# Opening of a hybrid decoder trunk: the first scale and shift as columns, and x turned ahead of them

## Chip, cores and metric

The kernel runs on one core of a Trainium2 chip. The metric is the device time of one launch in microseconds; smaller is better.

## The reference, cut to what matters

A trunk of two layers, each of three sub-layers (a SwiGLU feed-forward, a hybrid mixer, a second feed-forward), on 256 tokens of 1024 features in float32. Every sub-layer starts with the same two steps. The change touches them for the first feed-forward only:

```python
mod = silu(c) @ w_ada[i] + b_ada[i]                       # c is one vector of 1024
sh1, sc1, g1, ... = split(mod, 9)
h = rms_norm(x, norm_pre[i, 0]) * (1 + sc1) + sh1         # by token: x / rms(x), by feature: the rest
y = swiglu_ffn(h, w_ffn_in[i, 0], w_ffn_out[i, 0])
```

## The kernel before, in words

**Products.** Every large product is made of three products of rounded float32 (fp32r): a weight chunk (128x1024 in RAW) is split by ScalarE into a high half (WH, line 1348) and by VectorE into the rest (WL, line 1697), and activations likewise into HH and HL; high by high, high by low and low by high are summed in PSUM. TensorE needs 12 products of 512 columns for a chunk.

**The opening.** The first feed-forward goes through its first 12 chunks in the order FIRST_ORDER (lines 76 and 77): for each quarter q of the 1024 input features, the chunks of units 0, 1 and 2. So chunks 3q, 3q+1 and 3q+2 need only quarter q of h. Quarter q of scale and shift needs 16 slabs of w_ada (8 blocks of 128 rows, for scale and for shift), which the SP queue loads in pieces (`first_slabs`, line 682) between the weight chunks: chunks 2q and 2q+1 go out beside the slabs of quarter q.

**Scale and shift as rows.** `first_rows_of` (line 999) multiplies two or four of the eight row blocks on TensorE with the activated c as a stationary operand broadcast over 128 columns, so that each partition of PSUM bank 7 holds the same 512 numbers (256 of shift, 256 of scale). The other blocks are accumulated by VectorE in `first_steps` (line 1716, operations at line 1729), and one product with ones (line 1008) adds their sum over partitions. The norm's gain is spread over partitions by four one-row products (line 1317) at the very start.

**h by token.** VectorE makes x times root times gain (`first_x_pre`, line 1735), then for each quarter (1 + scale) times that (line 1748, twice) plus shift (line 1753, twice). TensorE turns the result by four transposes (`first_turn`, line 1019), ScalarE copies it rounded into HH (line 1423), and VectorE subtracts HH from the turned block for HL (line 1761). The turns of quarters 1 to 3 stand ahead of the last products of chunks 2, 5 and 8.

**Order.** All of it is written out by hand: each engine has its own program and waits on semaphores. VectorE: roots, steps of quarter 0, h of quarter 0, then for each quarter w_lo to chunk 3q, HL, w_lo of chunk 3q+1, steps of the next quarter, w_lo of chunk 3q+2, h of the next quarter (lines 2261 to 2280). ScalarE: squares and roots of x, a table load, then w_hi to chunk 3q and HH for each quarter. TensorE fills its waits ahead of the first chunk with products of ones (`kept_busy`, line 1309: 8, 6 and 1 of them). ACC and PSLAB hold sums and slabs; X and Y hold x and h by token. Eight chunks can be in RAW; SP issues chunk g + 8 when chunk g was used.

Of the kernel before, what the change touches and what calls it, by code (L numbers as in the profile page):

```python
# [11 lines left out]
ALU = mybir.AluOpType  # L12
# [305 lines left out]
def build(nc, x_d, c_d, w_ada, b_ada, norm_pre, norm_post, w_ffn_in, w_ffn_out, w_in, pool_w, w_ret_out, w_pool_out,  # L318
          w_ssm_out, w_fox_out, w_out, vecs_d, consts_d, out_d):
    with ExitStack() as ctx:  # L320
# [47 lines left out]
        EPS = SMALL[:, 16:17]  # L368
        DUMMY = SMALL[:, 17:18]
        _, dg_off = sb("rows_area", [P, TT, P])  # L370
        ZF = at("dt_by_feature", [P, T], F32, dg_off)
# [86 lines left out]
        def scaled(b, n):  # L458

            return n if b == 0 else 2 + 5 * (b - 1) + n  # L460

# [19 lines left out]
        first_used = sem("ada_first_used")  # L481
        first_rows = sem("first_rows_in_psum")
        first_pre = sem("first_pre_row_landed")
        first_pre_ps = sem("first_pre_row_in_psum")
        late_h = sem("late_h_by_token")
        ada_used = Signal(sem("ada_used"), 24)
# [129 lines left out]
        def _(sp):  # L616
# [50 lines left out]
            def pre_row(t):  # L667
                if t == 1:
                    sp.wait_ge(late_h, 6)
                else:  # L670
                    sp.wait_ge(f_ok, scaled(t - 1, 5))
                sp.dma_start(AROW[:], norm_pre[t // 3, t % 3, :].partition_broadcast(P)).then_inc(pre_landed.sem, 16)
# [18 lines left out]
            sp.dma_start(CS[:], c_d.rearrange("a (k p) -> p (a k)", p=P)).then_inc(c_landed, 16)  # L691
            sp.dma_start(AROW[0:1, :], norm_pre[0, 0:1, :]).then_inc(first_pre, 16)
            for tt in range(TT):
# [5 lines left out]
            first_slabs(0, 2)  # L699
            sp.dma_start(KC[:, 0:P], consts_d[:, 0:P]).then_inc(ident_landed, 16)  # L700
            for q in range(4):
                if q:
                    first_slabs(q, 0)
                chunk(2 * q)
                if q:
                    first_slabs(q, 1)
                chunk(2 * q + 1)
# [33 lines left out]
        def _(pe):  # L741
# [9 lines left out]

            def token_chunk(g, j, banks, hi, lo, kn, tts, lo_ready=None, ahead_of_last=None):

# [24 lines left out]
                for kk, tt in parts:  # L778
                    k = 2 * j + kk
                    if ahead_of_last is not None and (kk, tt) == parts[-1]:  # L780
                        ahead_of_last()
                    out = PS[:, banks + tt, :]
                    cs = slice(kk * HALF, (kk + 1) * HALF)
                    mm(out, hi[:, k, tok(tt)], wh[:, cs], start=(k == 0), stop=False)  # L784
                    mm(out, hi[:, k, tok(tt)], wl[:, cs], start=False, stop=False)  # L785
                    if lo_ready is None:
                        ins = lo_product(kk, tt)
# [6 lines left out]
            def ffn_in(s, c):  # L794
# [44 lines left out]
                if s == 0 and u == 0:  # L839
                    pe.wait_ge(hh_ok, h_parts(0, q + 1))  # L840

                    def ready():
                        pe.wait_ge(hl_ok.sem, hl_ok.at(0, q + 1))
                ahead = None
                if s == 0 and c in (2, 5, 8):
                    def ahead():
                        first_turn(c // 3 + 1)
                token_chunk(g, q, unit_banks(s, u), HH, HL, KD, (0, 1), ready, ahead).then_inc(w_used, 1)

# [148 lines left out]

            def first_rows_of(q):

                out = PS[:, 7, :].rearrange("p (n c) -> p n c", n=2)
                slabs = PSLAB[:].rearrange("p (n k) c -> p n k c", n=2)
                for i, k in enumerate(on_pe(q)):
                    pe.wait_ge(ada_first[piece_of(q, k)], 32)
                    mm(out, CS[:, k:k + 1].to_broadcast([P, P]), slabs[:, :, k, q * QUARTER:(q + 1) * QUARTER], start=(i == 0),
                       stop=False)
                pe.wait_ge(first_used, first_steps_of(q)[1])
                mm(out, ones, ACC[:, 0:2 * D].rearrange("p (n c) -> p n c", n=2)[:, :, q * QUARTER:(q + 1) * QUARTER],
                   start=False, stop=True).then_inc(first_rows if q < 3 else a_ps.sem, 1)

            def first_turn(q):

                for tt in range(TT):
                    if q == 0:
                        pe.wait_ge(f_ok, scaled(0, tt + 1))
                    else:
                        pe.wait_ge(late_h, 2 * (q - 1) + tt + 1)
                    for k in range(2):
                        ins = pe.transpose(PS[:, 6, k * T + tt * P:k * T + (tt + 1) * P],
                                           Y[:, tt, (2 * q + k) * P:(2 * q + k + 1) * P], ident)  # L1020
# [11 lines left out]
            def ffn(s):  # L1032
# [3 lines left out]
                for c in range(4 if s else 0, N_IN):  # L1036
# [3 lines left out]
                    if s == 0 and c in (2, 5, 8):  # L1040
                        first_rows_of(c // 3 + 1)
                    if s == 0 and c == 27:
# [271 lines left out]

            pe.wait_ge(first_pre, 16)
            for half in range(2):
                ins = mm(PS[:, 2 + half, :], ONE[0:1, 0:1].to_broadcast([1, P]), AROW[0:1, half * HALF:(half + 1) * HALF],
                         start=True, stop=True)
            ins.then_inc(first_pre_ps, 1)
            kept_busy(8)  # L1320
            first_rows_of(0)
            pe.wait_ge(xsq_ok.sem, xsq_ok.at(0, 4))
            pe.wait_ge(ident_landed, 16)
            kept_busy(6)
            first_turn(0)
            kept_busy(1)
            for s in range(SUBS):
# [7 lines left out]
        def _(act):  # L1335
# [83 lines left out]

            def first_h_hi(q):  # L1420

                act.wait_ge(t_ps, h_parts(0, q + 1))
                fn(HH[:, 2 * q:2 * q + 2, :], PS[:, 6, :].rearrange("p (k t) -> p k t", k=2), ACT.Copy).then_inc(hh_ok, 1)

# [245 lines left out]
            x_square(0, 0)  # L1670
            x_square(0, 1)
            fn(DUMMY[:], one, ACT.Silu)
            for q in range(4):
                split_to(3 * q)
                first_h_hi(q)
            for s in range(SUBS):
# [7 lines left out]
        def _(dve):  # L1684
# [30 lines left out]

            def first_steps(q):

                cs = slice(q * QUARTER, (q + 1) * QUARTER)
                acc = ACC[:, 0:2 * D].rearrange("p (n c) -> p n c", n=2)[:, :, cs]
                slabs = PSLAB[:].rearrange("p (n k) c -> p n k c", n=2)  # L1720
                if q == 0:
                    for n in range(2):
                        dve.wait_ge(bias_landed[n].sem, bias_landed[n].at(0, 16))
                for m in range(*first_steps_of(q)):
                    k = FIRST_STEPS[m][1]
# [5 lines left out]

            def first_x_pre(tt):

                dve.wait_ge(first_pre_ps, 1)
                chain(dve.scalar_tensor_tensor(Y[:, tt, :].rearrange("p (b n) -> p b n", b=2),
                                               X[:, tt, :].rearrange("p (b n) -> p b n", b=2), RB[:, tt:tt + 1],
                                               PS[:, 2:4, :], ALU.mult, ALU.mult))

            def first_h_full(q):

                cs = slice(q * QUARTER, (q + 1) * QUARTER)
                if q < 3:
                    dve.wait_ge(first_rows, q + 1)
                else:
                    dve.wait_ge(a_ps.sem, a_ps.at(0, 1))
                scaled_at = []
                for tt in range(TT):
                    ins = dve.scalar_tensor_tensor(Y[:, tt, cs], PS[:, 7, QUARTER:2 * QUARTER], 1.0, Y[:, tt, cs], ALU.add,
                                                   ALU.mult)
                    scaled_at.append(chain.mark(ins))  # L1750
                for tt in range(TT):
                    chain.need(scaled_at[tt])
                    dve.tensor_tensor(Y[:, tt, cs], Y[:, tt, cs], PS[:, 7, 0:QUARTER], ALU.add)\
                        .then_inc(late_h if q else f_ok, 1)
                if q == 3:
                    dve.sem_inc(a_ok.sem, 1)

            def first_h_lo(q):

                dve.wait_ge(hh_ok, h_parts(0, q + 1))  # L1760
                dve.tensor_tensor(HL[:, 2 * q:2 * q + 2, :], PS[:, 6, :].rearrange("p (k t) -> p k t", k=2),
                                  HH[:, 2 * q:2 * q + 2, :], ALU.subtract).then_inc(hl_ok.sem, 1)
# [498 lines left out]
            for tt in range(TT):  # L2261
                x_part(0, tt)
                x_root(0, tt)
                if tt == 0:
                    first_x_pre(0)
            first_steps(0)
            first_x_pre(1)
            first_h_full(0)
            for q in range(4):
# [4 lines left out]
                split_to(3 * q + 1)  # L2274
                first_steps(q + 1)
                split_to(3 * q + 2)
                if q == 2:
                    dve.wait_ge(first_used, len(FIRST_STEPS))
                    dve.sem_inc(ada_used.sem, ADA_FIRST)
                first_h_full(q + 1)  # L2280
            for s in range(SUBS):
# [108 lines left out]
```

## Time and profile before

| what | value |
|---|---|
| median of 3 runs | 1488.42 us (1487.47 to 1488.42) |
| the profiled execution, its own time | 1487.86 us |
| its span, first to last instruction | 1485.8 us |
| TensorE, VectorE, ScalarE, GpSimd busy | 99%, 78%, 55%, 4% |
| DMA | 342.94 MB, mean 231 GB/s |
| first product of chunk 0 | 17.93 us after the span's start |
| first product of chunk 9 (the last quarter of h) | 53.63 us |

The profiled execution takes 2.06 us more than its span, and 0.56 us less than the median. PE is TensorE, PEld its weight loads, DVE VectorE, ACT ScalarE, POOL GpSimd, SP the DMA queue. A product of 512 columns shows 0.39 us long, since its pipeline is included; what counts is the spacing of starts.

### The profile page before, as it was taken

What the parts mean: (1) busy time and instruction counts of PE and PEld (TensorE: products, weight loads), DVE (VectorE), ACT (ScalarE), POOL (GpSimd) and SP (SyncE); (2) the same over time, 40 slices, a digit from 0 to 9 for tenths busy, and PEclk for the clock granted to TensorE, in tenths of its full rate; (3) what the DMA queues carried; (4) which work ended last, traced back from release to release, by engine and by line L of the source; (5) the groups of instructions that cost most, each with busy time, mean ns of one, the idle gap of its engine ahead of it and who ended that gap; (6) DMA issues with size and microseconds to landing.
All of it is one profiled execution on the core that took longest, in us unless ns stands there. A gap on an engine that the chain in (4) does not pass through costs nothing.

```text
span 1485.8 us, 20504 instructions
## 1 busy us (share of the span) xinstructions
PE 1473.5 (99%) x7991; PEld 1259.6 (85%) x7991; DVE 1161.1 (78%) x1414; ACT 816.5 (55%) x1016; POOL 56.8 (4%) x56
## 2 busy tenths in 40 slices
PE   8999999999999999999999999999999999999998
PEld 5788889997988878888888888899888888888886
DVE  6888777867799878889787897776879988775663
ACT  4545465566563456556465564654746545664553
POOL 0000003200000000000000000050000000000000
PEclk9999999999999999999999999999999999999999
DMA  9899966556777847888768887665667787566652
GB/s 349 292 323 303 336 221 206 167 164 186 226 250 245 284 156 241 259 277 286 241 227 263 272 280 250 192 184 158 183 192 244 244 263 234 179 187 186 195 187 99
DMA packets 203623, 342.94 MB, mean 231 GB/s; under 512 B 18547, under 2 KB 118131, under 8 KB 203526
## 3 DMA queue, kind: packets, MB, share of 16 engines
q1 hardware_dynamic: 185382, 275.56, 58.2%
q10 hardware_dynamic: 18144, 66.07, 13.4%
q8 instruction: 63, 1.03, 0.3%
q14 instruction: 34, 0.28, 0.1%
HBM read 340.53 MB, written 1.05 MB: 230 GB/s over the span
## 4 chain that ended last, share of the span: by engine, by line
PE 97%; DVE 2%; ACT 1%; issue 1%; DMA 0%; DVEq 0%; ACTq 0%
PE ps L819 12%; PE ps L784 11%; PE ps L775 11%; PE ps L785 11%; PE ps L933 6%; PE ps L935 6%; PE ps L934 6%; PE ps L824 6%; PE ps L1274 5%; PE ps L1275 5%; PE ps L1276 5%; PE ps L867 3%; PE ps L973 1%; PE ps L860 1%; PE ps L1146 1%
## 5 line engine op out<-in xcount | busy, mean ns | idle before, releaser
L1697 DVE TENSOR_TENSOR w_lo<-w_raw,w_hi 128x1024 fp32r<-128x1024 f32 x480 | 574.7, 1219 | 100.7 <-ACT w_hi L1348 100.2
L1348 ACT ACTIVATE w_hi<-w_raw 128x1024 fp32r<-128x1024 f32 x490 | 504.7, 1051 | 259.5 <-DMA w_raw<-in_w_ffn_out 70.5
L784 PE MATMUL ps<-w_hi,h_both 128*128 128x512 f32 x586 | 231.0, 394 | 0.0
L785 PE MATMUL ps<-w_lo,h_both 128*128 128x512 f32 x586 | 228.3, 390 | 0.0
L775 PE MATMUL ps<-w_hi,h_both 128*128 128x512 f32 x586 | 227.6, 390 | 0.0
L819 PE MATMUL ps<-h_both,w_hi 128*128 128x512 f32 x768 | 206.6, 394 | 0.0
L1274 PE MATMUL ps<-h_both,w_hi 128*128 128x256 f32 x640 | 182.6, 285 | 0.0
L1276 PE MATMUL ps<-h_both,w_lo 128*128 128x256 f32 x640 | 181.1, 283 | 0.0
L1275 PE MATMUL ps<-h_both,w_hi 128*128 128x256 f32 x640 | 181.1, 283 | 0.0
L1713 DVE SCALAR_TENSOR_TENSOR ada_acc<-ada_slab,c_silu,ada_acc 128x1024 f32<-128x1024 f32 x128 | 163.7, 1279 | 5.7 <-DMA ada_slab<-in_w_ada 5.7
L819 PEld LDWEIGHTS ps<-h_both,w_hi 128*128 128x128 f32 x768 | 132.9, 189 | 19.2
L933 PE MATMUL ps<-w_hi,act_hi 128*128 128x512 f32 x352 | 137.6, 391 | 0.0
L935 PE MATMUL ps<-w_hi,act_lo 128*128 128x512 f32 x352 | 137.0, 389 | 0.0
L934 PE MATMUL ps<-w_lo,act_hi 128*128 128x512 f32 x352 | 137.0, 389 | 0.0
L784 PEld LDWEIGHTS ps<-w_hi,h_both 128*128 128x128 f32 x586 | 110.1, 188 | 24.1 <-DVE w_lo L1697 2.4
L775 PEld LDWEIGHTS ps<-w_hi,h_both 128*128 128x128 f32 x586 | 110.0, 188 | 23.4
L785 PEld LDWEIGHTS ps<-w_lo,h_both 128*128 128x128 f32 x586 | 110.2, 188 | 21.8
L824 PEld LDWEIGHTS ps<-h_both,w_lo 128*128 128x128 f32 x768 | 114.5, 189 | 14.2
L1274 PEld LDWEIGHTS ps<-h_both,w_hi 128*128 128x128 f32 x640 | 122.7, 192 | 0.6 <-issue 0.3
L1275 PEld LDWEIGHTS ps<-h_both,w_hi 128*128 128x128 f32 x640 | 122.8, 192 | 0.2
L1276 PEld LDWEIGHTS ps<-h_both,w_lo 128*128 128x128 f32 x640 | 122.7, 192 | 0.0
L824 PE MATMUL ps<-h_both,w_lo 128*128 128x256 f32 x768 | 118.3, 281 | 0.0
(310 smaller groups left out, 1860.2 us busy)
## 6 DMA issues: line engine op xcount, KB each, us to landing
w_raw<-in_w_ffn_in SPq DMA_DIRECT2D x352, 256.0 KB, 3.8
w_raw<-in_w_in SPq DMA_DIRECT2D x168, 512.0 KB, 3.7
ada_slab<-in_w_ada ACTq DMA_DIRECT2D x126, 512.0 KB, 4.6
w_raw<-in_w_ffn_out SPq DMA_DIRECT2D x88, 512.0 KB, 4.2
w_raw<-in_w_ssm_out SPq DMA_DIRECT2D x16, 512.0 KB, 4.7
w_raw<-in_w_out SPq DMA_DIRECT2D x16, 512.0 KB, 3.4
ada_slab_first<-in_w_ada SPq DMA_DIRECT2D x14, 512.0 KB, 7.2
w_raw<-in_w_pool_out SPq DMA_DIRECT2D x8, 512.0 KB, 3.6
```

The lines of the kernel that those rows point to most:

```text
L775: return mm(PS[:, banks + tt, :], lo[:, k, tok(tt)], wh[:, kk * HALF:(kk + 1) * HALF], start=False, stop=(k == kn - 1))
L784: mm(out, hi[:, k, tok(tt)], wh[:, cs], start=(k == 0), stop=False)
L785: mm(out, hi[:, k, tok(tt)], wl[:, cs], start=False, stop=False)
L819: ins = mm(PS[:, bank, :], wh[:, cs], HB[:, k, :, :], start=(k == 0), stop=(k == KD - 1))
L824: ins = mm(PS[:, bank, 0:T], wl[:, cs], HH[:, k, :], start=False, stop=False)
L933: mm(out, hi[:, k, tok(tt)], wh[:, cs], start=first, stop=False)
L934: mm(out, hi[:, k, tok(tt)], wl[:, cs], start=False, stop=False)
L1274: mm(out, wh[:, cs], HH[:, k, :], start=(k == 0 and t % 2 == 0), stop=False)
L1275: mm(out, wh[:, cs], HL[:, k, :], start=False, stop=False)
L1276: ins = mm(out, wl[:, cs], HH[:, k, :], start=False, stop=(k == KD - 1 and t % 2 == 1))
L1348: fn(WH[:, n % N_HI, 0:width], RAW[:, n % N_RAW, 0:width], ACT.Copy).then_inc(w_hi, 1)
L1697: dve.tensor_tensor(WL[:, n % N_RAW, 0:width], RAW[:, n % N_RAW, 0:width], WH[:, n % N_HI, 0:width], ALU.subtract).then_inc(w_lo, 1)
```

## The change

Scale and shift become columns, one number for each partition (feature). TensorE takes the slab as the stationary operand and the activated c as one moving column: for each row block of a quarter four products, for shift and scale by two feature blocks of 128, into 16 columns of bank 7. x times root is made by ScalarE, turned by TensorE without waiting for scale and shift, and full h is made from the turned block with a scale and a bias for each partition: high half and full h by ScalarE (high half of quarter 0 by VectorE), into HH and into Y, which is free by then. The gain is loaded as 1024 single elements (NORMC) behind the identity, and the load of its row is dropped.

```diff
@@ -367,6 +367,9 @@
         DUMMY = SMALL[:, 17:18]
+        NORMC, _ = sb("first_norm_columns", [P, KD])
+        SCALEC, _ = sb("first_scale_columns", [P, KD])
+        SHIFTC, _ = sb("first_shift_columns", [P, KD])
         _, dg_off = sb("rows_area", [P, TT, P])
...
@@ -457,7 +460,7 @@
-            return n if b == 0 else 2 + 5 * (b - 1) + n
+            return 5 * (b - 1) + n
...
@@ -665,9 +670,7 @@
             def pre_row(t):
-                if t == 1:
-                    sp.wait_ge(late_h, 6)
-                else:
+                if t > 1:
                     sp.wait_ge(f_ok, scaled(t - 1, 5))
...
@@ -689,7 +692,6 @@
             sp.dma_start(CS[:], c_d.rearrange("a (k p) -> p (a k)", p=P)).then_inc(c_landed, 16)
-            sp.dma_start(AROW[0:1, :], norm_pre[0, 0:1, :]).then_inc(first_pre, 16)
             for tt in range(TT):
...
@@ -698,6 +700,7 @@
             sp.dma_start(KC[:, 0:P], consts_d[:, 0:P]).then_inc(ident_landed, 16)
+            sp.dma_start(NORMC[:], norm_pre[0, 0:1, :].rearrange("a (k p) -> p (a k)", p=P)).then_inc(first_pre, 16)
             for q in range(4):
...
@@ -841,11 +842,7 @@
                         pe.wait_ge(hl_ok.sem, hl_ok.at(0, q + 1))
-                ahead = None
-                if s == 0 and c in (2, 5, 8):
-                    def ahead():
-                        first_turn(c // 3 + 1)
-                token_chunk(g, q, unit_banks(s, u), HH, HL, KD, (0, 1), ready, ahead).then_inc(w_used, 1)
+                token_chunk(g, q, unit_banks(s, u), HH, HL, KD, (0, 1), ready).then_inc(w_used, 1)
...
@@ -996,25 +993,29 @@
-            def first_rows_of(q):
-
-                out = PS[:, 7, :].rearrange("p (n c) -> p n c", n=2)
-                slabs = PSLAB[:].rearrange("p (n k) c -> p n k c", n=2)
-                for i, k in enumerate(on_pe(q)):
+            def column_group(q):
+
+                return [(PS[:, 7, 4 * q + 2 * n + b:4 * q + 2 * n + b + 1], n, q * QUARTER + b * P) for n in range(2)
+                        for b in range(2)]
+
+            def first_products_of(q, ks):
+
+                for k in ks:
                     pe.wait_ge(ada_first[piece_of(q, k)], 32)
-                    mm(out, CS[:, k:k + 1].to_broadcast([P, P]), slabs[:, :, k, q * QUARTER:(q + 1) * QUARTER], start=(i == 0),
-                       stop=False)
+                    for i, (out, n, col) in enumerate(column_group(q)):
+                        mm(out, PSLAB[:, 8 * n + k, col:col + P], CS[:, k:k + 1], start=(k == 0 and i == 0), stop=False)
+
+            def first_sums_of(q):
+
                 pe.wait_ge(first_used, first_steps_of(q)[1])
-                mm(out, ones, ACC[:, 0:2 * D].rearrange("p (n c) -> p n c", n=2)[:, :, q * QUARTER:(q + 1) * QUARTER],
-                   start=False, stop=True).then_inc(first_rows if q < 3 else a_ps.sem, 1)
+                for i, (out, n, col) in enumerate(column_group(q)):
+                    ins = mm(out, ACC[:, n * D + col:n * D + col + P], one, start=False, stop=(i == 3))
+                ins.then_inc(first_sums if q < 3 else a_ps.sem, 1)
...
+                pe.wait_ge(x_rooted, 4 if q else 2)
                 for tt in range(TT):
-                    if q == 0:
-                        pe.wait_ge(f_ok, scaled(0, tt + 1))
-                    else:
-                        pe.wait_ge(late_h, 2 * (q - 1) + tt + 1)
                     for k in range(2):
...
@@ -1038,7 +1039,9 @@
                     if s == 0 and c in (2, 5, 8):
-                        first_rows_of(c // 3 + 1)
+                        first_turn(c // 3 + 1)
+                        first_products_of(c // 3 + 1, on_pe(c // 3 + 1))
+                        first_sums_of(c // 3 + 1)
                     if s == 0 and c == 27:
...
@@ -1312,18 +1315,15 @@
-            pe.wait_ge(first_pre, 16)
-            for half in range(2):
-                ins = mm(PS[:, 2 + half, :], ONE[0:1, 0:1].to_broadcast([1, P]), AROW[0:1, half * HALF:(half + 1) * HALF],
-                         start=True, stop=True)
-            ins.then_inc(first_pre_ps, 1)
-            kept_busy(8)
-            first_rows_of(0)
-            pe.wait_ge(xsq_ok.sem, xsq_ok.at(0, 4))
+            kept_busy(14)
+            first_products_of(0, (0, 1))
+            kept_busy(3)
+            first_products_of(0, (4,))
             pe.wait_ge(ident_landed, 16)
-            kept_busy(6)
             first_turn(0)
-            kept_busy(1)
+            first_products_of(0, (6,))
+            first_sums_of(0)
+            kept_busy(3)
             for s in range(SUBS):
...
@@ -1417,10 +1417,29 @@
-            def first_h_hi(q):
+            def first_by_root(tt, c0, c1):
+
+                act.wait_ge(first_roots, tt + 1)
+                fn(Y[:, tt, c0:c1], X[:, tt, c0:c1], ACT.Copy, scale=RB[:, tt:tt + 1]).then_inc(x_rooted, 1)
+
+            def first_h(q):
...
                 act.wait_ge(t_ps, h_parts(0, q + 1))
-                fn(HH[:, 2 * q:2 * q + 2, :], PS[:, 6, :].rearrange("p (k t) -> p k t", k=2), ACT.Copy).then_inc(hh_ok, 1)
+                act.wait_ge(first_columns, q + 1)
+                for b in range(2):
+                    k = 2 * q + b
+                    if q:
+                        ins = fn(HH[:, k, :], PS[:, 6, b * T:(b + 1) * T], ACT.Identity, scale=SCALEC[:, k:k + 1],
+                                 bias=SHIFTC[:, k:k + 1])
+                if q:
+                    ins.then_inc(hh_ok, 1)
+                else:
+                    act.wait_ge(hh_ok, 1)
+                for b in range(2):
+                    k = 2 * q + b
+                    ins = fn(Y[:, b, q * QUARTER:(q + 1) * QUARTER], PS[:, 6, b * T:(b + 1) * T], ACT.Identity,
+                             scale=SCALEC[:, k:k + 1], bias=SHIFTC[:, k:k + 1])
+                ins.then_inc(first_full, 1)
...
@@ -1669,10 +1688,14 @@
             x_square(0, 1)
+            first_by_root(0, 0, QUARTER)
+            first_by_root(1, 0, QUARTER)
             fn(DUMMY[:], one, ACT.Silu)
+            first_by_root(0, QUARTER, D)
+            first_by_root(1, QUARTER, D)
             for q in range(4):
                 split_to(3 * q)
-                first_h_hi(q)
+                first_h(q)
             for s in range(SUBS):
...
@@ -1713,15 +1736,15 @@
-            def first_steps(q):
+            def first_steps(q, m0, m1):
...
                 slabs = PSLAB[:].rearrange("p (n k) c -> p n k c", n=2)
-                if q == 0:
+                if m0 == 0:
                     for n in range(2):
                         dve.wait_ge(bias_landed[n].sem, bias_landed[n].at(0, 16))
-                for m in range(*first_steps_of(q)):
+                for m in range(m0, m1):
                     k = FIRST_STEPS[m][1]
...
@@ -1729,36 +1752,35 @@
-            def first_x_pre(tt):
-
-                dve.wait_ge(first_pre_ps, 1)
-                chain(dve.scalar_tensor_tensor(Y[:, tt, :].rearrange("p (b n) -> p b n", b=2),
-                                               X[:, tt, :].rearrange("p (b n) -> p b n", b=2), RB[:, tt:tt + 1],
-                                               PS[:, 2:4, :], ALU.mult, ALU.mult))
-
-            def first_h_full(q):
-
-                cs = slice(q * QUARTER, (q + 1) * QUARTER)
+            def first_scales(q):
+
                 if q < 3:
-                    dve.wait_ge(first_rows, q + 1)
+                    dve.wait_ge(first_sums, q + 1)
                 else:
                     dve.wait_ge(a_ps.sem, a_ps.at(0, 1))
-                scaled_at = []
-                for tt in range(TT):
-                    ins = dve.scalar_tensor_tensor(Y[:, tt, cs], PS[:, 7, QUARTER:2 * QUARTER], 1.0, Y[:, tt, cs], ALU.add,
-                                                   ALU.mult)
-                    scaled_at.append(chain.mark(ins))
-                for tt in range(TT):
-                    chain.need(scaled_at[tt])
-                    dve.tensor_tensor(Y[:, tt, cs], Y[:, tt, cs], PS[:, 7, 0:QUARTER], ALU.add)\
-                        .then_inc(late_h if q else f_ok, 1)
+                if q == 0:
+                    dve.wait_ge(first_pre, 16)
+                ks = slice(2 * q, 2 * q + 2)
+                dve.tensor_copy(SHIFTC[:, ks], PS[:, 7, 4 * q:4 * q + 2])
+                dve.scalar_tensor_tensor(SCALEC[:, ks], PS[:, 7, 4 * q + 2:4 * q + 4], 1.0, NORMC[:, ks], ALU.add, ALU.mult)\
+                    .then_inc(first_columns, 1)
                 if q == 3:
...
+            def first_h_hi():
+
+                dve.wait_ge(t_ps, h_parts(0, 1))
+                dve.wait_ge(first_columns, 1)
+                for b in range(2):
+                    ins = dve.tensor_scalar(HH[:, b, :], PS[:, 6, b * T:(b + 1) * T], SCALEC[:, b:b + 1], SHIFTC[:, b:b + 1],
+                                            ALU.mult, ALU.add)
+                ins.then_inc(hh_ok, 1)
+
             def first_h_lo(q):
...
                 dve.wait_ge(hh_ok, h_parts(0, q + 1))
-                dve.tensor_tensor(HL[:, 2 * q:2 * q + 2, :], PS[:, 6, :].rearrange("p (k t) -> p k t", k=2),
+                dve.wait_ge(first_full, q + 1)
+                dve.tensor_tensor(HL[:, 2 * q:2 * q + 2, :], Y[:, :, q * QUARTER:(q + 1) * QUARTER],
                                   HH[:, 2 * q:2 * q + 2, :], ALU.subtract).then_inc(hl_ok.sem, 1)
...
@@ -2261,23 +2283,22 @@
                 x_root(0, tt)
-                if tt == 0:
-                    first_x_pre(0)
-            first_steps(0)
-            first_x_pre(1)
-            first_h_full(0)
+                dve.sem_inc(first_roots, 1)
+                first_steps(0, 2 * tt, 2 * tt + 2)
+            first_scales(0)
+            first_h_hi()
             for q in range(4):
...
                 split_to(3 * q + 1)
-                first_steps(q + 1)
+                first_steps(q + 1, *first_steps_of(q + 1))
                 split_to(3 * q + 2)
...
                     dve.sem_inc(ada_used.sem, ADA_FIRST)
-                first_h_full(q + 1)
+                first_scales(q + 1)
             for s in range(SUBS):
...
```

What is left out: names of semaphores, and the parameter by which a turn stood ahead of a chunk's last products.

## Rows read from the trace of the kernel before

**Rows 1.** The page, part 1: busy time, share of the span, instructions.
```profile
PE 1473.5 (99%) x7991; PEld 1259.6 (85%) x7991; DVE 1161.1 (78%) x1414; ACT 816.5 (55%) x1016; POOL 56.8 (4%) x56
```
**Rows 2.** Waits of TensorE's weight loads, whole span: total us, times, longest.
```profile
PEld ps L784 <- DVE w_lo L1697: 2.4, 3, 0.8
```
**Rows 3.** Timeline of the opening: start, us, engine, line, operation, idle before.
```profile
9.30 1.28 ACT L1672 ACT_TABLE_LOAD   x1
...
9.91 0.16 DVE L1791 SCALAR_TENSOR_TENSOR small_columns<-small_columns 128x1 f32<-128x1 f32 x1
10.11 3.32 DVE L1729 SCALAR_TENSOR_TENSOR ada_acc<-ada_slab_first,c_silu,ada_acc 128x512 f32<-128x512 f32 x4
...
13.35 1.27 DVE L1735 SCALAR_TENSOR_TENSOR y_tok<-x_res,small_columns,ps 128x1024 f32<-128x1024 f32 x1
...
13.77 1.06 ACT L1348 ACTIVATE w_hi<-w_raw 128x1024 fp32r<-128x1024 f32 x1 [2.97 <-DMA w_raw<-in_w_ffn_in]
...
15.33 0.76 DVE L1748 SCALAR_TENSOR_TENSOR y_tok<-ps,y_tok 128x256 f32<-128x256 f32 x2 [0.71 <-PE ps L1008]
...
16.00 0.74 DVE L1753 TENSOR_TENSOR y_tok<-y_tok,ps 128x256 f32<-128x256 f32 x2
...
17.28 0.60 ACT L1423 ACTIVATE h_both<-ps 128x512 fp32r<-128x512 f32 x1 [2.45 <-PE ps L1019]
...
17.93 1.20 PE L759 MATMUL ps<-w_hi,h_both 128*128 128x512 f32 x4 [0.47 <-ACT h_both L1423]
```
**Rows 4.** Timeline of the later quarters, 20 to 54 us, same columns.
```profile
20.00 5.03 DVE L1729 SCALAR_TENSOR_TENSOR ada_acc<-ada_slab_first,c_silu,ada_acc 128x512 f32<-128x512 f32 x6
...
26.22 0.19 PEld L784 LDWEIGHTS ps<-w_hi,h_both 128*128 128x128 f32 x1 [0.81 <-DVE w_lo L1697]
...
41.69 1.05 ACT L1348 ACTIVATE w_hi<-w_raw 128x1024 fp32r<-128x1024 f32 x1
...
43.92 5.03 DVE L1729 SCALAR_TENSOR_TENSOR ada_acc<-ada_slab_first,c_silu,ada_acc 128x512 f32<-128x512 f32 x6
...
46.35 1.06 ACT L1348 ACTIVATE w_hi<-w_raw 128x1024 fp32r<-128x1024 f32 x1 [3.60 <-DMA w_raw<-in_w_ffn_in]
...
48.87 1.22 DVE L1697 TENSOR_TENSOR w_lo<-w_raw,w_hi 128x1024 fp32r<-128x1024 f32 x1
...
53.63 1.19 PE L759 MATMUL ps<-w_hi,h_both 128*128 128x512 f32 x4
```
**Rows 5.** Windows: us, busy of PE, PEld, DVE, ACT, POOL, clock, DMA share, GB/s.
```profile
2.00:3.00 1.00, 0.00 (x0) 0.00 (x0) 0.00 (x0) 0.32 (x3) 1.00 (x2) 1.00 1.24 65
30.00:35.00 5.00, 5.00 (x23) 4.13 (x22) 4.02 (x6) 1.64 (x2) 0.00 (x0) 1.00 1.09 382
```
**Rows 6.** Chain that ended last, TensorE's part: start, us, line, count.
```profile
7.12 3.71 PE ps L1312 x8
...
15.22 1.31 PE ps L1312 x6
...
20.95 0.23 PE ps L784
...
23.67 1.72 PE ps L1005 x4
...
28.56 0.45 PE ps L1019 x4
```
**Rows 7.** Timeline in the mixer: one-column products with 128x128 stationary operands.
```profile
413.29 0.50 PE L1181 MATMUL ps<-small_columns,squares_ssd 128*128 128x1 f32 x4
413.65 0.49 PE L784 MATMUL ps<-w_hi,h_both 128*128 128x512 f32 x1
```
**Rows 8.** Timeline of the SP queue at the start: the row that is dropped.
```profile
1.24 0.47 SPq L692 DMA_DIRECT2D scale_row<-in_norm_pre  x1
```
**Rows 9.** Groups by line and shape: busy us, mean ns, idle before.
```profile
L1556 ACT ACTIVATE xbc<-ps,vectors 128x256 f32<-128x256 f32 x24 | 11.6, 565 | 16.7 <-PE ps L1276 16.7
...
L2152 DVE TENSOR_SCALAR scratch_t<-ps,vectors 128x256 f32<-128x256 f32 x8 | 3.3, 478 | 5.8 <-PE ps L1132 5.8
```

More of the change, by code:

```diff
@@ L481, in build @@
         first_used = sem("ada_first_used")
[L482 to L485, printed above, removed]
+        first_sums = sem("first_columns_in_psum")
+        first_pre = sem("first_pre_columns_landed")
+        first_columns = sem("first_scale_and_shift_ready")
+        first_roots = sem("first_roots_ready")
+        x_rooted = sem("first_x_by_root")
+        first_full = sem("first_h_full")
         ada_used = Signal(sem("ada_used"), 24)
@@ L750, in tok, with token_chunk @@
                 return slice(tt * P, (tt + 1) * P)
-            def token_chunk(g, j, banks, hi, lo, kn, tts, lo_ready=None, ahead_of_last=None):
+            def token_chunk(g, j, banks, hi, lo, kn, tts, lo_ready=None):
                 parts = [(kk, tt) for kk in range(2) for tt in tts]
@@ L779, in token_chunk @@
                     k = 2 * j + kk
-                    if ahead_of_last is not None and (kk, tt) == parts[-1]:
-                        ahead_of_last()
                     out = PS[:, banks + tt, :]
```

## The prediction, made before any run of the changed kernel

> **What bounds the kernel now.** Start with the busy shares: TensorE is busy for 1473.5 of 1485.8 us [rows 1], so only work that it drops or idle time of its own can be won. Next come the waits of its weight loads: what holds the feed-forward's products is w_lo, three times and 0.8 us at most, all in the opening [rows 2, 4]. Then the timeline of the opening: the first product of chunk 0 starts at 17.93 us and that of chunk 9, the last that needs a new quarter of h, at 53.63 us [rows 3, 4]. Behind that point the waits show TensorE waiting for no transfer. So the change is worth what it moves that second point, and about 1 us of 1488 is at stake for each us there. A change of 0.2% is 3.0 us, about what a measurement here can tell from none.
>
> The opening has a second bound. From about 4 us until 52 us the DMA engines are full (share 1.09, 382 GB/s) [rows 5], and w_hi of chunk 8 waits for its landing until 46.35 us [rows 4].
>
> **Quarter 0, before.** The root of the second half of x is ready at 10.07 us; four steps run from 10.11 to 13.43; then VectorE still multiplies x (1.27 us), waits for the sums, and passes four times over h, from 15.33 to 16.74; turn, copy (0.60 us) and the first product at 17.93 follow in a row [rows 3]. From the end of the steps to the first product: 4.50 us.
>
> **Quarter 0, after.** The norm row leaves SP's queue ahead of x: 0.47 us of issuing [rows 8], so x and all behind it may come up to 0.5 us earlier. Its four one-row products and both passes of x times root (1.27 us each) go too. I take roots and first steps as 0.5 us earlier.
> - VectorE: two steps (0.83 us each, 3.32 for four [rows 3]) from about 9.0 when the first slabs are there, four small operations for the second root (some 0.2 us each, nearest row 0.16 [rows 3]) to 11.5, two steps to 13.2.
> - TensorE: the last eight sum instructions. The nearest row is products of one column with a 128x128 stationary operand: four take 0.36 us from start to next start, 0.09 each [rows 7]. Eight: 0.7 us, with latency 1.1, so 14.3 us. Two small VectorE operations: 14.65. High half by VectorE: two operations of 128x256 from PSUM, 0.41 us each (3.3 us for 8 [rows 9]): 15.5 us.
> - ScalarE, behind the second root at 11.5: quarter 0 of x by root, about 0.48 us (nearest row 11.6 us for 24 [rows 9]), the table load 1.28 us [rows 3], the rest of x, twice about 0.95 us (an estimate: w_hi takes 1.06 for 1024 columns [rows 3]), and only then w_hi of chunk 0, 1.06 us. Ends at 16.4 us. Before, w_hi was done at 14.83, with 3 us to spare.
>
> So ScalarE's queue ends last, not the columns: first product at about 16.4, 1.5 us earlier. HL of quarter 0 also waits for ScalarE's full h, two operations of 0.48 us, hidden by w_lo of chunk 0 (1.22 us [rows 4]) on VectorE.
>
> **Quarters 1 to 3.** TensorE: before, four row instructions took 1.72 us [rows 6], 0.43 each, and two sum instructions of the same size come to 0.86, together 2.58; after, 16 and 8 instructions at 0.09, 2.2 us; at 0.12 they would be 2.9. I take zero to 0.4 us saved each. VectorE drops 1.4 us each (two lines [rows 3]) and gets two small operations, about 0.4. ScalarE gets four operations, 1.9 us, for one of 0.60; high half is ready after 1.0 us and no longer waits for a turn, so products of chunks 3, 6 and 9 need not wait for it (0.4 us each before).
>
> But the chain between quarters is w_lo of chunk 3q+1, six steps (5.03 us), w_lo of chunk 3q+2 (1.22), then products. For quarter 1 the steps ran from 20.00 to 25.03, and chunk 2 waited to 26.22 [rows 4]. They can start earlier only as far as slabs are there: by bytes, the second half of quarter 1's slabs is 3.15 MB behind chunk 0, which landed at 13.77 [rows 3], at 0.382 MB/us [rows 5] thus at 22.0; three steps follow (2.5 us): 24.5 at best. For quarter 3 the steps stand behind w_lo of chunk 7, whose w_hi ran at 41.69 [rows 4]; chunk 8 landed by 46.35, and 2.1 MB lie between, so chunk 7 landed about 40.9. At most 0.8 us can be won there.
>
> **The price of the gain's columns.** NORMC is 1024 transfers of 4 bytes in the full stretch of the DMA. The like of it is the load of c: in the window from 2.0 to 3.0 us the 16 engines are busy 1.24 us each while only 65 GB/s move [rows 5]; less 0.2 for those bytes, which are x's (0.065 MB at 0.382), that is 1.0 us of all 16. Bounds: 0 (hidden between large packets) and 1.2 us. I take 1.0: with x earlier by 0.5 everything behind lands 0.5 us later than before. The Trainium skill, DMA: Bandwidth & Descriptors, Rules for kernel authors, says that a non-contiguous last dimension becomes one descriptor for each element, and its Bandwidth section gives about 10.5 ns for a packet, by which an estimate of the 64 packets of an engine would be 0.67 us; the sum would then be 0.3 us better.
>
> With it: quarter 1's steps end at about 25.0 (no gain), chunk 2 starts with w_lo at 26.2 as before and ends 0.45 earlier, as no turn (0.45 us [rows 6]) stands in it. Chunk 6 starts about 1 us earlier. w_hi of chunk 7 starts at 41.4 instead of 41.69, w_lo ends at 43.7 (43.9 before), six steps to 48.8, w_lo of chunk 8 to 50.0, chunk 8 (12 products by 0.23 us, the spacing in [rows 6], 2.73 in all) to 52.8: chunk 9 starts 0.8 us earlier. ScalarE's queue behind the last h, which sets the first turn of the activation, is 1.1 us earlier. **Sum: 1.1 us** less of the profiled 1487.86, 1486.8; the median stands 0.56 above: 1487.3.
>
> **Rivals.**
> - *Bound by transfers (15%).* If NORMC costs the whole 1.2 us and x comes no earlier, w_lo of chunk 7 ends 0.4 us later than before and the steps with it; what the missing turn gives back is used up. The same end if the columns, being thin work, leave TensorE slow at chunk 0: before, one-row products and then eight of 512 columns had a spacing of 0.46 us (3.71 for 8), six later ones 0.22 [rows 6], its two levels of 1.2 and 2.4 GHz, while the granted clock reads 1.00 in all windows. At the slow level chunk 0 costs up to 2.4 us more, of which the wait for the steps at 25 us takes most. 1488.4 to 1489.4.
> - *Slower (6%): the clock falls in every quarter.* Place: turn, 24 thin products and the wait for the steps, 3 to 4 us ahead of chunks 2, 5 and 8, where broad products of 512 columns stood. Price: a chunk at 0.43 us for a product costs 12 x 0.2 = 2.4 us more. It decides from the point where two of three quarters fall: three give 7.2 - 1.1 = 6.1 us more, 1494.5. Against: thin products in the mixer are followed by products at full spacing (0.09 us, next to normal ones [rows 7]), though those are only four. The Trainium skill, TensorE: Matmul & The Clock Gate, PE-mode transpose, says that transposes do not count as activity for the clock; no row here shows that alone. By it, this rival gets its chance.
> - *Faster than 0.2% (6%): the DMA does not bind.* Then from 16.4 us on TensorE goes on without waits: nine chunks by 2.73 us, three turns 0.45 [rows 6], three times 2.2 us of columns: chunk 9 at 49.0 to 49.8 instead of 53.63, 3.8 us or more. Against: landings of chunks 7 and 8 [rows 4]. 1484.4.
> - *No effect (3%).* The earlier start is spent in the wait for the steps of quarter 1, and nothing is won later. 1488.4.
>
> **How the numbers follow.** Forecast 70%, a gain of 0.2 to 2.9 us, most likely 1.1: 1487.3. With the transfer rival and the neutral one 88% lie within 0.2%; I give 87% there, 7% faster, 6% slower. The range from 1485.2 to 1490.2 holds the forecast's case with both ends of NORMC and of the column products, and the transfer rival; 12% or a little more is outside.
>
> **What the profile after would show.** Right: first product near 16.4 us, released by w_hi of chunk 0 and not by columns; HL never last; the three steps runs ending at about 25, 36.5 and 48.8 us; chunk 8 waiting for w_lo; chunk 9 at 52.5 to 53.1 us; landing of chunk 0 about 0.5 us later than 13.77. Wrong: column instructions spaced over 0.12 us or products behind them at 0.43 us (clock); landings earlier than before; a first product before 15.8 us (the columns, not ScalarE, end last); a wait for a transfer that was none before; any difference behind 60 us.

## The result, and the profile after

Measured: 1491.96 us median (1488.50 to 1494.13, 22 runs) against 1488.45 (1487.47 to 1489.34, 22 runs) for the kernel before; ratio 1.0024, 95% interval 1.0018 to 1.0030. The change makes the kernel slower by 0.24%. The forecast was 1487.3 with a range from 1485.2 to 1490.2; it was wrong, and the case that came true is the slower rival, the clock. Every time given as a result is a median of several executions, and a profile shows one of them.

The profiled execution took 1491.60 us, its span is 1489.6. The windows of the changed kernel (us, busy time of PE, PEld, DVE, ACT and POOL, granted clock, DMA share, GB/s) show what none of the kernel before shows:

```profile
12.50:20.00 7.50, 7.50 (x32) 6.17 (x32) 4.59 (x9) 5.75 (x8) 0.00 (x0) 0.58 1.08 378
20.00:27.00 7.00, 7.00 (x44) 6.16 (x43) 6.07 (x8) 2.12 (x2) 0.00 (x0) 0.96 1.09 382
27.00:31.00 4.00, 4.00 (x14) 3.29 (x14) 2.25 (x5) 2.88 (x5) 0.00 (x0) 0.57 1.09 385
31.00:40.00 9.00, 9.00 (x55) 7.83 (x53) 6.58 (x8) 2.12 (x2) 0.00 (x0) 1.00 1.09 388
40.00:45.00 5.00, 5.00 (x18) 4.05 (x18) 3.37 (x6) 2.88 (x5) 0.00 (x0) 0.66 1.04 401
45.00:53.00 8.00, 8.00 (x51) 7.01 (x49) 5.47 (x7) 2.12 (x2) 0.00 (x0) 1.00 1.09 382
53.00:58.00 5.00, 5.00 (x18) 4.07 (x18) 3.43 (x6) 4.29 (x7) 1.85 (x2) 0.66 0.25 89
58.00:70.00 12.00, 12.00 (x60) 9.90 (x60) 9.62 (x11) 8.93 (x12) 0.00 (x0) 1.00 0.66 201
```

Four of the same windows in the kernel before:

```profile
12.50:20.00 7.50, 7.03 (x27) 4.37 (x26) 6.40 (x11) 3.40 (x4) 0.00 (x0) 1.00 1.09 384
...
27.00:31.00 4.00, 4.00 (x20) 2.99 (x19) 2.91 (x6) 1.54 (x2) 0.00 (x0) 1.00 1.09 385
...
40.00:45.00 5.00, 5.00 (x25) 3.81 (x24) 3.76 (x5) 1.55 (x2) 0.00 (x0) 1.00 1.04 396
...
53.00:58.00 5.00, 5.00 (x22) 3.81 (x21) 4.13 (x4) 5.00 (x6) 0.95 (x1) 1.00 0.54 174
```

The clock is down in four stretches, one for each quarter, where it was 1.00 before. TensorE is busy all through the last three, so what is lost in them is the share below 1.00 times the length: 0.43 x 4 + 0.34 x 5 + 0.34 x 5 = 5.1 us. The chain that ended last (start, us, line) shows where they begin, here for quarter 1:

```profile
24.93 1.68 PE ps L1006 x16
26.61 0.92 PE ps L1012 x8
27.53 0.64 PE ps L785
28.17 0.43 PE ps L786
28.59 0.43 PE ps L778
29.02 0.43 PE ps L785
29.45 0.43 PE ps L786
29.88 0.43 PE ps L778
30.30 0.43 PE ps L785
30.73 0.30 PE ps L786
31.03 0.23 PE ps L778
```

The 24 column instructions run at 0.105 us each (1.68 for 16), and the products right behind them have the spacing of 1.2 GHz, 0.43 us, until it is 0.23 again, 2.4 GHz. Behind the columns of quarters 2 and 3 two and five products still pass at 0.23 us before the same fall. Where the kernel before has 12 products at 0.23 [rows 6], seven or eight here cost 0.2 us more. The timeline of the first quarter and of chunk 9:

```profile
13.61 1.74 ACT L1423 ACTIVATE y_tok<-x_res,small_columns 128x768 f32<-128x768 f32 x2
...
13.96 1.84 PE L1012 MATMUL ps<-small_columns,ada_acc 128*128 128x1 f32 x8
...
15.26 1.04 ACT L1348 ACTIVATE w_hi<-w_raw 128x1024 fp32r<-128x1024 f32 x1
...
16.17 1.00 DVE L1775 TENSOR_SCALAR h_both<-ps,first_scale_columns,first_shift_columns 128x256 fp32r<-128x256 f32 x2
...
20.44 1.06 ACT L1348 ACTIVATE w_hi<-w_raw 128x1024 fp32r<-128x1024 f32 x1 [1.19 <-DMA w_raw<-in_w_ffn_in]
...
57.27 1.45 PE L762 MATMUL ps<-w_hi,h_both 128*128 128x512 f32 x4
```

Chunk 9 starts at 57.27 us instead of 53.63 [rows 4], 3.6 us later, and the whole difference of the spans is 3.8 us. Nothing behind 60 us adds to it. The waits of the weight loads up to 62 us are now three, none of them for w_lo or for the steps [rows 2]:

```profile
PEld ps L1315 <- issue: 3.3, 1, 3.3
PEld ps L1006 <- DMA ada_slab_first<-in_w_ada: 1.2, 1, 1.2
PEld ps L762 <- DVE h_both L1775: 0.7, 1, 0.7
```

From 17.3 us on TensorE waits for nobody, and it did not help: for part of the time it is its own bound, at half its clock. That the waits are gone is in part a result of that slowness; with the clock at 1.00 (the first experiment) it waits again, 1.1 us in all for w_lo and 0.3 us for the steps.

### The profile page after: what moved, and what is told of

It reads as the page before. It is cut to its first block, busy times and chain, and to the rows that moved or that the text cites. A ratio compares the mean times of both kernels' runs of the same rounds, so it can differ in the third digit from the quotient of the medians.

```text
span 1489.6 us, 20688 instructions
## 1 busy us (share of the span) xinstructions
PE 1476.9 (99%) x8076; PEld 1273.1 (85%) x8076; DVE 1154.7 (78%) x1406; ACT 823.1 (55%) x1030; POOL 56.7 (4%) x56
## 4 chain that ended last, share of the span: by engine, by line
PE 97%; DVE 2%; DMA 0%; issue 0%; ACT 0%; SPq 0%; DVEq 0%; ACTq 0%
PE ps L820 12%; PE ps L785 11%; PE ps L778 11%; PE ps L786 11%; PE ps L930 6%; PE ps L932 6%; PE ps L931 6%; PE ps L825 6%; PE ps L1277 5%; PE ps L1278 5%; PE ps L1279 5%; PE ps L864 3%; PE ps L970 1%; PE ps L857 1%; PE ps L1006 1%; PE ps L1149 1%
```

## The experiments

Theories: **clock** (one-column products let TensorE fall to 1.2 GHz in each quarter), **transfers** (the 1024 single elements of the gain put the landings back), **work** (the added instructions and the longer way to HH cost the time themselves).

**Columns made 128 wide.** The operand that moves is repeated; instructions, stationary operands and results stay.

```diff
-mm(out, PSLAB[:, 8 * n + k, col:col + P], CS[:, k:k + 1], ...)
+mm(out, PSLAB[:, 8 * n + k, col:col + P], CS[:, k:k + 1].to_broadcast([P, 128]), ...)
-ins = mm(out, ACC[:, n * D + col:n * D + col + P], one, ...)
+ins = mm(out, ACC[:, n * D + col:n * D + col + P], one.to_broadcast([P, 128]), ...)
```

(`out` is 128 columns of bank 7 for each, and VectorE reads the first of them.)

> The changed kernel with every product of a column widened: the moving operand is c (or one) repeated 128 times instead of one column, same stationary operands, same number of instructions. Theory clock (the thin products let TensorE fall to 1.2 GHz in front of chunks 2, 5 and 8, and 6 to 8 of the 12 products behind them take 0.43 us instead of 0.23): clock 1.00 in the three stretches, 4 to 5 us less than the changed kernel, chunk 9 near 52.8 us, about 1487.3, under before. Theory transfers (the 1024 single elements put all landings of the opening 1.2 us back): nothing changes here, 1491 to 1492. Theory work (more instructions of TensorE and a longer way through ScalarE to HH): the same or slower, since 128 columns cost at least as much as one.

Measured 1486.77 us (1486.25 to 1488.05, 11 runs), before 1488.12; ratio 0.9991 (0.9982 to 1.0000). Same windows, and the chain at quarter 2:

```profile
12.50:20.00 7.50, 6.73 (x42) 5.31 (x41) 4.70 (x8) 5.48 (x8) 0.00 (x0) 1.00 1.06 368
...
27.00:31.00 4.00, 4.00 (x19) 3.27 (x18) 2.81 (x5) 2.88 (x5) 0.00 (x0) 1.00 1.09 385
...
40.00:45.00 5.00, 5.00 (x23) 4.13 (x23) 3.55 (x5) 1.71 (x3) 0.00 (x0) 1.00 1.04 401
...
53.00:58.00 5.00, 4.88 (x22) 3.72 (x20) 4.15 (x5) 5.00 (x6) 0.00 (x0) 1.00 0.83 269
```
```profile
35.68 1.79 PE ps L1006 x16
37.47 0.89 PE ps L1013 x8
38.36 0.24 PE ps L785
38.60 0.23 PE ps L786
```

128 columns cost 0.112 us an instruction where one column cost 0.105, 0.1 us in 16, and the clock stays at 1.00. Chunk 9 starts at 52.28 us, 5.0 before the changed kernel. Theory work is out: the same instructions take 5.2 us less. Theory transfers is out as the cause: the gather of the gain is still there. The new places of the columns in bank 7 are not what helped either: in two kernels further on (one quarter thin, the others wide) one-column products write to these places and the clock falls.

**Broad products between the thin ones.**

```diff
-first_turn(c // 3 + 1)
-first_products_of(c // 3 + 1, on_pe(c // 3 + 1))
+pe.wait_ge(first_full, c // 3 + 1)
+for k in on_pe(c // 3 + 1):
+    first_products_of(c // 3 + 1, (k,))
+    spare_products(2)
 first_sums_of(c // 3 + 1)
+first_turn(c // 3 + 1)
```

These are two products of 512 columns behind each of the two blocks of columns, four a quarter, in quarters 1 to 3; quarter 0 stays thin. TensorE also waits for full h of the quarter before, and the turn moves behind the sums, so this edit changes more than one thing.

> The changed kernel with two products of 512 columns of ones behind each of the two blocks of columns of quarters 1 to 3 (four a quarter), and the turn behind the sums. Theory clock: the broad products are activity between the thin ones, the clock stays or falls for fewer products; they cost 4 x 0.22 = 0.9 us a quarter, 2.6 in all, and give back up to 4.9: 1489.5 to 1490.5 if all is given back. Theory transfers or theory work: 2.6 us slower than the changed kernel, about 1494.5.

Measured 1493.32 us (1489.26 to 1498.17, 10 runs), before 1488.12; ratio 1.0035 (1.0023 to 1.0047). The profiled execution, 1490.35 us, holds the clock in quarters 1 to 3 (0.23 us behind the columns; only quarter 0's fall is left) and lies where the clock theory put it. Other runs are up to 7.8 us above it, and their mean granted clock is lower, 0.991 in the slowest against 0.997. So four broad products hold the clock in some executions and not in others; as a remedy it failed.

**The gain turned instead of gathered.**

```diff
-sp.dma_start(NORMC[:], norm_pre[0, 0:1, :].rearrange("a (k p) -> p (a k)", p=P))
+sp.dma_start(AROW[0:KD, 0:P], norm_pre[0, 0, :].rearrange("(k p) -> k p", p=P))
+pe.transpose(PS[:, 4, 0:KD], AROW[0:KD, 0:P], ident[0:KD, 0:KD])
+dve.tensor_copy(NORMC[:], PS[:, 4, 0:KD])
```

> The changed kernel with the gain loaded as 8 rows of 128 numbers and turned into columns by one transpose, instead of 1024 single elements. Theory transfers: chunks 2, 3 and 5 land 1.2 us earlier (w_hi at 19.2, 23.3, 31.5 us) and the end comes 1 us or more earlier. Theory clock: TensorE waits for no transfer behind 17.3 us in the changed kernel, so landings come earlier and the end moves by under 0.5 us; the three stretches at 1.2 GHz stay.

Measured 1491.53 us (1486.75 to 1494.55, 9 runs), before 1488.12; ratio 1.0019 (1.0007 to 1.0030), not told apart from the changed kernel. The profiled execution had w_hi of chunk 3 at 23.12 us instead of 24.54, and still took 1493.04: in it the clock fell earlier, was 0.50 from 12.5 to 20 us, and chunk 0 started at 19.27 us; the next three windows of 5 us have 0.79, 0.90 and 0.76. The weights come earlier and TensorE waits for no transfer, as expected.

**Thin and wide products added to the kernel before.** Behind the rows of quarters 1 to 3, twelve products of the identity by one column of c, or by that column repeated 128 times; the results are not used.

```diff
+pe.wait_ge(hl_ok.sem, hl_ok.at(0, c // 3))
+for i in range(12):
+    mm(PS[:, 6, i:i + 1], ident, CS[:, 0:1], start=True, stop=True)                   # thin
+    mm(PS[:, 6, 0:P], ident, CS[:, 0:1].to_broadcast([P, P]), start=True, stop=True)  # wide, instead
```

> The kernel before with twelve products of one column (24 instructions, 128x128 stationary) added behind the rows of quarters 1 to 3; their results are used by nobody. Theory clock: besides 24 x 0.105 = 2.5 us a quarter the clock falls and the chunk behind is 1.6 us longer: 3 x 4.1 = 12 us slower, 1500.5. Theory work (instructions alone): 3 x 2.5 = 7.6, 1496, and the products behind keep 0.23 us.

> The kernel before with 12 thin products in each of quarters 1 to 3, again, as the partner of the next one. Theory clock: 1 to 4 us slower than its partner, with runs far apart. Theory work: equal to its partner.

> The kernel before with 12 added products of 128 columns in each of quarters 1 to 3: the same number of instructions and stationary operands as the thin ones. Theory clock: only their own time, 3 x 2.6 = 7.8 us over the kernel before, 1496, runs close together, clock 1.00. Theory work: the same time as with thin ones, 1498 to 1499.

Thin: 1498.55 us (1496.48 to 1499.67, 4 runs), ratio 1.0070 (1.0055 to 1.0085), and again 1498.25 (1495.62 to 1500.01, 4 runs), 1.0064 (1.0050 to 1.0077). Wide, on the chip of the second: 1495.82 (1495.69 to 1496.67, 4 runs), 1.0050 (1.0036 to 1.0064). The wide ones cost 7.3 us, their own time as expected; the thin ones 2.4 us more by the medians. With four runs each the two intervals overlap; but six of the eight thin runs are slower than every wide one, and their mean clock is 0.997 to 0.999. One thin execution, at clock 1.00, took 1495.62. In the first thin profile the fall came in quarter 3 alone:

```profile
54.78 2.57 PE ps L1044 x24
57.35 0.34 PE ps L784
57.69 0.24 PE ps L785
57.92 0.23 PE ps L775
58.15 0.23 PE ps L784
58.39 0.42 PE ps L785
58.80 0.43 PE ps L775
```

In the wide profile every window up to 65 us reads 1.00. So thin products alone bring the fall, in a kernel that has nothing else of the change, and without a turn just ahead of them. My 12 us for the clock theory were too many: here the fall comes in some quarters only. That the broad row products just ahead of the thin ones are the reason is a guess.

**Which quarters.** Only quarter 0 wide, and only quarters 1 to 3 wide.

```diff
+def width(q):
+    return 1 if q else 128      # or: 128 if q else 1
```

> Only the columns of quarter 0 are 128 wide, those of quarters 1 to 3 one column as in the changed kernel. Theory clock by quarter (each quarter's thin stretch costs its own fall): chunk 0 runs at 0.23 us and starts chunk 2 some 0.8 us earlier, the falls in front of chunks 2, 5 and 8 stay: 0.5 to 1 us under the changed kernel, about 1491. Rival, one cause at the start (a clock that was slow at chunk 0 is what makes the later ones fall): all falls go, 1487.

> Only the columns of quarters 1 to 3 are 128 wide, those of quarter 0 thin. Theory clock by quarter: the stretch from 13 to 21 us stays at 1.20 GHz, which costs 0.8 us at chunk 2, and the other three falls go, some 4 us: 1487.5 to 1488. Rival, one cause at the start: the falls stay, 1491 to 1492.

Quarter 0 wide: 1489.35 us (1488.62 to 1491.21, 10 runs), ratio 1.0008 (0.9999 to 1.0017). Quarters 1 to 3 wide: 1487.60 (1487.12 to 1490.42, 10 runs), ratio 0.9999 (0.9990 to 1.0008), before 1488.47. A later fall does not need the first one: with a good quarter 0 the products behind quarters 1 and 3 still stood at 0.43 us (from 27.95 and 51.62 us), behind quarter 2 not; with only quarter 0 thin, the first eight products of chunk 0 took 2.07 and 1.68 us (1.07 a four at full speed) and those of all later chunks were at full speed. My split was off: a wide quarter 0 gave 2.6 us by the medians, not 0.5 to 1. In its profile one of the three later falls is missing, but that is its fastest run. The parts do not add up either: against the widened kernel a thin quarter 0 costs 0.8 us and thin quarters 1 to 3 cost 2.6, together 3.4, while all four thin cost 5.2. These runs are of different chips, and what couples the quarters is open.

**32 columns.**

> All columns 32 wide instead of 1 or 128. Theory clock: what counts is how much of the time the array has columns moving through; with 32 of 128 it has so for a quarter of a product's 0.105 us, so some falls stay: between 1487 and 1491.5, the clock of the three stretches between that of the changed and of the widened kernel. Theory that any product of more than one column is enough: 1486.8 and clock 1.00.

Measured 1487.36 us (1486.43 to 1493.03, 10 runs), before 1488.47; ratio 0.9998 (0.9989 to 1.0007). The profiled execution had one fall, products at 0.43 us from 26.43 to 29.8 us. About half of the runs are as fast as with 128 columns, the others up to 6 us slower, and in seven of the ten the mean clock is 0.998 or less. So 32 columns do not hold the clock reliably; nothing between 32 and 128 was tried.

**Both.** The widened columns and the turned gain.

> The widened columns together with the gain as 8 rows turned by one transpose. With the clock held, TensorE and VectorE wait for landings again (VectorE's steps of quarter 1 for slabs at 23.1 us, ScalarE's w_hi of chunk 7 at 40.9). Theory transfers matter once the clock is held: landings 1.2 us earlier, the steps of quarter 1 end 0.5 us earlier and w_hi of chunk 7 by 1 us: 0.5 to 1 us under the widened kernel, 1485.9 to 1486.3. Theory that the chain of splits and steps alone binds: no difference to the widened kernel, 1486.8.

> The widened kernel again, beside the one with the turned gain on the same chip. Both theories of the transfers: about 1.3 us under the kernel before.

> The widened kernel with the turned gain again, same chip as the widened one. Theory transfers matter once the clock is held: 0.5 to 1 us under it. Theory that splits and steps alone bind: within 0.3 us of it.

Both changes: 1485.91 us (1485.55 to 1487.56, 11 runs), ratio 0.9985 (0.9976 to 0.9993), and again 1486.20 (1485.78 to 1487.47, 11 runs), 0.9985 (0.9976 to 0.9994). Widened alone on the chip of the second: 1486.78 (1486.29 to 1489.63, 11 runs), 0.9992 (0.9983 to 1.0000), before 1488.51. By the medians the gain's load is worth 0.6 us once the clock holds; the two intervals overlap, so that size is an indication. The timelines of the first pair show ScalarE's w_hi of chunks 2 and 3 in the widened kernel and then with both:

```profile
20.40 1.06 ACT L1349 ACTIVATE w_hi<-w_raw 128x1024 fp32r<-128x1024 f32 x1 [1.45 <-DMA w_raw<-in_w_ffn_in]
24.48 1.06 ACT L1349 ACTIVATE w_hi<-w_raw 128x1024 fp32r<-128x1024 f32 x1 [3.02 <-DMA w_raw<-in_w_ffn_in]
```
```profile
18.97 1.06 ACT L1353 ACTIVATE w_hi<-w_raw 128x1024 fp32r<-128x1024 f32 x1 [0.16 <-DMA w_raw<-in_w_ffn_in]
23.06 1.06 ACT L1353 ACTIVATE w_hi<-w_raw 128x1024 fp32r<-128x1024 f32 x1 [3.03 <-DMA w_raw<-in_w_ffn_in]
```

1.4 us earlier. By 32.6 us both kernels wait for the same landing, and only 0.1 us is left. These two profiles are of different chips. In the second pair, on one chip, w_hi of chunk 3 moves by 0.2 us only:

```profile
23.45 1.06 ACT L1349 ACTIVATE w_hi<-w_raw 128x1024 fp32r<-128x1024 f32 x1 [3.03 <-DMA w_raw<-in_w_ffn_in]
```
```profile
23.25 1.06 ACT L1353 ACTIVATE w_hi<-w_raw 128x1024 fp32r<-128x1024 f32 x1 [3.03 <-DMA w_raw<-in_w_ffn_in]
```

What does not vary is one window of the DMA. First the widened kernel, then both changes, on that chip:

```profile
10.00:12.50 2.50, 2.50 (x22) 2.42 (x21) 2.06 (x7) 0.73 (x2) 0.00 (x0) 1.00 1.16 321
```
```profile
10.00:12.50 2.50, 2.50 (x22) 2.42 (x21) 2.08 (x7) 0.52 (x2) 0.00 (x0) 1.00 1.10 379
```

Every profile with the gather has 320 to 322 GB/s there, every one without it 378 to 380. That is 0.15 MB less in 2.5 us, by my estimate 0.4 us at 382 GB/s. Up to 23 us the two kernels moved 326 and 332 GB/s, which is the same amount. Both changes together beat the kernel before and the changed one.

## Why the prediction was wrong, point by point

- **The bound** was read rightly: what the second point of the opening (the first product of chunk 9) moved, the end moved: 3.6 us and 3.8, or with wide columns -1.35 and -1.3.
- **Quarter 0.** ScalarE ended w_hi of chunk 0 at 16.30 us (16.4 forecast). But the columns ended last, at 17.17: the eight sum instructions took 1.71 us, 0.21 each, at the low clock, not 0.7, and VectorE's two operations 1.00, not 0.85. First product 17.22 instead of 16.4. With wide columns and the clock at 1.00 it is 16.92, and the columns still end last (16.86 us; w_hi at 16.02): the steps end at 13.14 us, but TensorE starts the sums at 14.44 only, busy until then with the turn and the last block's columns. The prediction had the sums start with the end of the steps, so "ScalarE's queue ends last" fails with the clock at 1.00 too, by 0.5 us.
- **Price of the columns.** 0.105 us an instruction, inside 0.09 to 0.12. As durations the terms were right. The step that failed is the one behind them: the sum has chunk 8 at "12 products by 0.23 us" behind the columns, and the runs showed seven or eight of the 12 at 0.43 us in each of the three quarters, 5.1 us. It rested on "thin products in the mixer are followed by products at full spacing", from which I gave the clock 6%. Four instructions in a stream of broad ones [rows 7] say nothing of 24. A row of the opening was closer, eight broad products still at 0.46 us behind one-row products of 3.7 us, and I used it for chunk 0 only. It is no proof: the widened kernel starts with broad products, and its first 14 take 6.22 us, 0.44 each.
- **The rival** named place and cause, and its price was too high: 2.4 us a quarter for a whole chunk. Seven or eight of 12 products were slow, about 1.7 us, 5.1 in the three; chunk 0's cost about 0.75 at chunk 2 (27.53 against 26.80 us, in the chains). The starts of products against the widened kernel add up: chunk 2 is 0.6 us later (27.39 and 26.78), chunk 3 2.15, chunk 6 3.7, chunk 9 5.0. The widened kernel is 1.35 us ahead of the kernel before at chunk 9, which leaves the 3.6 measured there.
- **The forecast's own sum** holds where its assumption does: with the clock kept the kernel was 1.35 us faster by the medians (1.1 forecast), chunk 9 at 52.28 us (52.8), the steps of quarter 1 ended at 25.6 us (25.0), those of quarter 3 at 48.1 (48.8). Part of that is luck: chunk 2 started 0.56 us later than before, not at the same time, and the later quarters won more than forecast (chunk 9 0.5 us earlier than the sum has it); the misses offset each other.
- **The gain's single elements.** Forecast 0.5 us later landings, net; measured 1.24 for chunk 2 in the changed kernel (20.44 instead of 19.20), with x 0.25 us earlier instead of 0.5. But other kernels with the same gather have this w_hi at 19.36 to 20.40 us (one even at 21.84), so a single profile does not give the price; the DMA window gives an estimate of 0.4 us, less than the 1.0 of the sum. The Trainium skill's figure (DMA: Bandwidth & Descriptors, Bandwidth) came to an estimate of 0.67; no run here decides between these. It made no difference to this verdict.
- **The Trainium skill's rule on transposes and the clock** (TensorE: Matmul & The Clock Gate, PE-mode transpose) gave this rival its chance, and the runs do not bear it out as the cause: the turns stayed in the widened kernel, and its clock held; with thin products added to the kernel before it fell with no turn just ahead. Whether the turns add to the fall no run here shows.

## What to carry to other kernels

A TensorE that reads as busy can still lose its clock: before broad products are replaced by thin ones of the same duration (here 24 instructions, 2.6 us), look at the granted clock and at the spacing of the products behind them. Where columns are wanted, repeat the moving operand; here 128 columns cost 0.007 us an instruction more than one and were worth 5 us. A gather of single elements in a stretch where the DMA is full takes time from the transfers behind it; the rows that were loaded and turned left the same DMA window at 379 GB/s.

## What the runs showed of the hardware that was not expected

- A busy TensorE did not keep its clock: PE was busy for the whole of 20 to 58 us in the changed kernel, and its clock fell three times. With the same instructions moving 128 columns instead of one it stayed at 1.00.
- With thin products runs of one kernel differ by more than any other part of this change: 1488.50 to 1494.13 us, in step with the mean granted clock, 0.996 in the fastest and 0.992 in the slowest; with 128 columns it is 0.999 to 1.000 and 1486.25 to 1489.63 (22 runs on two chips). A single profile can show a fall too few: that of the kernel with broad products between the thin ones was 3 us under its median.
- For the same reason medians of the kernels between (32 columns, broad products, one quarter wide) reflect how often the clock fell in those runs, and the smaller differences among them are not settled.
